# Fifteen rows of the first tile's expert sum scaled and added by GpSimd between its gathers, where VectorE added eleven

## What is computed

```python
def peer(h, w_query, sub_keys, expert_u, expert_v):
    ...
        idx = jnp.take_along_axis(cand_i, best_pos, axis=-1)
        gate = jax.nn.softmax(best_s, axis=-1)
        u = expert_u[idx]
        act = jax.nn.gelu(jnp.einsum('thkd,td->thk', u, x_blk), approximate=False)
        vsel = expert_v[idx]
        return jnp.einsum('thk,thkd->td', (gate * act).astype(vsel.dtype), vsel)
    ...
h = h + mix
h = h + peer(rmsnorm(h, norm_ffn[i]), ...)
```

## Time and profile before

| | us |
|---|---|
| median of 3 executions | 1581.6 |
| lowest, highest | 1579.9, 1583.37 |
| the profiled execution, its own time | 1584.37 |
| its span, first to last instruction | 1582.4 |

### The profile page before, as it was taken

The page is one execution under the profiler, slowest core; times in us unless marked ns, Lnnn a source line. Parts: engine busy times, 40 slices in busy tenths (PEclk is TensorE's granted clock), DMA queues, the critical chain, the costliest instruction groups (busy, mean ns, idle before and its releaser), DMA issues.

```text
span 1582.4 us, 14473 instructions
## 1 busy us (share of the span) xinstructions
PE 1348.0 (85%) x4096; PEld 666.3 (42%) x4096; DVE 973.4 (62%) x2432; ACT 537.7 (34%) x1639; POOL 564.0 (36%) x532
## 2 busy tenths in 40 slices
PE   7999899889775997889998699788899887777776
PEld 5555465445332443333565244333365432332222
DVE  3327498988774444763477755574557788554544
ACT  2324232323233223562323323564322323332322
POOL 1001355464342332434443233344333343343330
PEclk9999999999998999989999899999999999899999
DMA  9317999999999999999999999999999999999995
GB/s 382 142 53 292 371 405 421 421 421 421 421 421 422 420 421 421 419 404 409 421 421 421 420 421 422 421 407 386 423 421 420 422 420 422 422 421 422 421 421 218
DMA packets 85230, 620.39 MB, mean 392 GB/s; under 512 B 10368, under 2 KB 10368, under 8 KB 11424
## 3 DMA queue, kind: packets, MB, share of 16 engines
q0 software_dynamic: 74768, 551.65, 84.3%
q1 hardware_dynamic: 9792, 67.51, 10.4%
q10 hardware_dynamic: 592, 0.31, 0.1%
HBM read 618.38 MB, written 1.05 MB: 391 GB/s over the span
## 4 chain that ended last, share of the span: by engine, by line
PE 41%; DMA 39%; DVE 9%; ACT 7%; issue 3%; SPq 0%; POOL 0%; ACTq 0%; DVEq 0%; POOLq 0%
DMA arena<-in_peer_uv_dram,hnT 28%; PE banks L544 25%; DMA raw<-in_peer_uv_dram,hnT 6%; PE banks L571 5%; PE banks L424 5%; DMA work<-in_peer_uv_dram,hnT 3%; DVE arena L1430 3%; PE banks L692 2%; DMA rt<-in_diff_lambda_k_dram 2%; ACT g_e L934 2%; ACT hnT L923 1%; PE banks L516 1%; DMA spare<-in_peer_uv_dram,hnT 1%; DVE raw L1430 1%; ACT hnT L918 1%
## 5 line engine op out<-in xcount | busy, mean ns | idle before, releaser
L544 PE MATMUL banks<-arena,g_e 128*128 128x512 f32 x1184 | 576.6, 621 | 129.2 <-ACT g_e L934 127.7
L350 POOL DMA_INDIRECT arena<-in_peer_uv_dram,hnT x299 | 321.2, 1074 | 510.4 <-PE banks L544 498.5
L544 PEld LDWEIGHTS banks<-arena,g_e 128*128 128x128 f32 x1184 | 218.2, 196 | 404.6 <-issue 216.9
L1430 DVE CUSTOM_DVE_ANT_0 arena<-arena,hrows 128x1024 f32<-128x1024 f32 x209 | 254.1, 1223 | 154.5 <-DMA arena<-in_peer_uv_dram,hnT 148.3
L918 ACT ACTIVATE hnT<-hnT 128x2 f32<-128x2 f32 (+2 forms) x241 | 48.9, 203 | 698.6 <-DVE hnT L1430 698.4
L544 PE MATMUL banks<-raw,g_e 128*128 128x512 f32 x424 | 207.1, 620 | 40.2 <-ACT g_e L934 36.3
L350 POOL DMA_INDIRECT raw<-in_peer_uv_dram,hnT x106 | 116.5, 1099 | 180.5 <-PE banks L544 178.4
L934 ACT ACTIVATE g_e<-ident,hnT 128x128 f32<-128x128 f32 x501 | 172.8, 393 | 1.9 <-ACT hnT L923 0.6
L1430 DVE CUSTOM_DVE_ANT_0 arena<-arena,banks 128x1024 f32<-128x1024 f32 x90 | 109.6, 1220 | 85.4 <-DMA arena<-in_peer_uv_dram,hnT 85.3
L544 PEld LDWEIGHTS banks<-raw,g_e 128*128 128x128 f32 x424 | 78.0, 196 | 132.5 <-issue 78.0
L1430 DVE CUSTOM_DVE_ANT_0 raw<-raw,hrows 128x1024 f32<-128x1024 f32 x80 | 97.5, 1223 | 56.7 <-DMA raw<-in_peer_uv_dram,hnT 56.6
(11 more groups left out here) (244 smaller groups left out, 1302.7 us busy)
## 6 DMA issues: line engine op xcount, KB each, us to landing
arena<-in_diff_in_dram SPq DMA_DIRECT2D x24, 1024.0 KB, 9.9
arena<-in_peer_query_dram SPq DMA_DIRECT2D x16, 1024.0 KB, 12.1
arena<-in_gla_in_dram POOLq DMA_DIRECT2D x5, 2048.0 KB, 20.6
arena<-in_peer_query_dram SPq DMA_DIRECT2D x4, 2048.0 KB, 10.5
arena<-in_diff_out_dram SPq DMA_DIRECT2D x8, 1024.0 KB, 10.1
arena<-in_peer_uv_dram,hnT POOLq DMA_INDIRECT x299
work<-in_gla_out_dram POOLq DMA_DIRECT2D x2, 2048.0 KB, 40.2
arena<-in_gla_in_dram SPq DMA_DIRECT2D x2, 1024.0 KB, 12.3
```

Of the source, the lines that this page charges most:

```text
L350: pool.indirect_dma_start(pair(n), None, table, bass.IndirectOffsetOnAxis(ap=places[:, o:o + 1].bitcast(u32), axis=0)).then_inc(S(f"pair_l ...
L544: last = nc.tensor.matmul(bank(2 * (tile % NT) + half), diags[:, slot * P:(slot + 1) * P], v_row(n)[:, half * 512:(half + 1) * 512], start ...
L1430: V.tensor_tensor_reduce(out=u_row(n), in0=u_row(n), in1=normed, scale=1.0, scalar=0.0, op0=ALU.mult, op1=ALU.add, accum_out=dots[:, o:o + ...
```

## The change

`ADDED` becomes fifteen rows, 3, 11, 19, ... 115. VectorE's `added` goes. GpSimd instead multiplies the `v` half in place with the weights and adds it onto `h[:, 0, :]`, right behind gather n+8 (behind gather 9 for row 3); the next gather is the one that writes into that row's buffer.

```diff
-ADDED = [n for n in range(16, 80, 6)]
+ADDED = [n for n in range(3, SLOTS - 8) if n % 8 == 3]
+ADD_BEHIND = {n + (6 if n < 8 else 8): n for n in ADDED}
...
                     ).then_inc(S(f"pair_loaded_{HOME[n]}"), 16)
+                late = ADD_BEHIND.get(n)
+                if late is not None:
+                    if added_to(late) > 1:
+                        pool.wait_ge(S("v_added"), added_to(late) - 1)
+                    pool.wait_ge(S("weighted"), late + 1)
+                    wait_landed(pool, late)
+                    pool.tensor_scalar(v_row(late), v_row(late), weights[:, late:late + 1], None, ALU.mult
+                                       ).then_inc(S("v_scaled"), 1)
+                    pool.wait_ge(S("v_scaled"), added_to(late))
+                    pool.tensor_tensor(h[:, 0, :], h[:, 0, :], v_row(late), ALU.add).then_inc(S("v_added"), 1)
...
-            def added(n):
...
-                    for n in ADDED:
-                        if SUM_T[n] == ticks:
-                            added(n)
```

More of the change, by code:

```diff
@@ L1432, in dot @@
                                        ).then_inc(S("u_dotted"), 1)
-            def added(n):
-                if added_to(n) > 1:
-                    dve.wait_ge(S("v_added"), added_to(n) - 1)
-                dve.wait_ge(S("weighted"), n + 1)
-                o = n % PICKS
-                V.scalar_tensor_tensor(out=h[:, 0, :], in0=v_row(n), scalar=weights[:, o:o + 1], in1=h[:, 0, :],
-                                       op0=ALU.mult, op1=ALU.add).then_inc(S("v_added"), 1)
             ticks = settled = 0
```

## The result

The changed kernel takes 1591.0 us (median of 6 runs, 1587.8 to 1592.65), the kernel before beside it 1582.6 us (6 runs, 1579.9 to 1583.4). The ratio is 1.0049 with an interval of 1.0038 to 1.0060: **slower by 8.4 us**. The forecast was 1584.9 us and the range ended at 1590.0, so it came out on the slower side, as the forecast had it, and two and a half times as far (8.4 us where the forecast added 3.3). The profiled execution took 1592.65 us with a span of 1590.7 us; before it was 1584.37 us with 1582.4 us.

The account below looks back on a forecast made before the run. The prediction took the DMA stream at 421 GB/s as the bound: 1581.6 us plus 3.3 at gather 20, with VectorE's lost additions and the other fourteen pairs at nothing, gave 1584.9 us; range 1581.2 to 1590.0.

Parts of the forecast that it names:

- the first term: At gather 20, row 11's scale and add (4.2 us alone) would widen the DMA hole by 3.3 us, ends 0.3 to 6.9.
- the prediction's hold-up: GpSimd's scale, add and next gather wait for VectorE's dots: 1.0 us on average, at best 0, at worst 3.3.
- the cover of 1.2 us: Transfers still queued ahead of gather 20 would hide 1.2 us of its 4.5 us delay.
- the second term: Row 3's pair delays gather 10 by about 4 us, covered by 12.4 us of transfer in gathers 5 to 9.
- if gathers 17 to 19 moved: Sign in the profile after that would show the prediction wrong: these gathers starting at other times than before.
- the third term: Later pairs cost nothing: cover is 4.5 us at gather 35 and 8.4 at gather 99, and GpSimd catches up between pairs.
- the 3.3: Lateness in us of the DMA stream after gather 20's hole, counted as extra cover for later pairs.
- Rival 2: VectorE becomes the first tile's bound, as GpSimd's reads hold up its dots: 1589 to 1591 us, chance 0.14.
- Rival 1: The pair is short or meets no dot, 2.8 to 3.5 us: 1582 to 1583 us, the same; chance 0.19.
- Rival 3: TensorE's relief from rows 3 and 11 shows, each giving 1.8 us back: 1578 us, chance 0.07.

Follow-up runs that it names:

- e1: Kernel before with no row added by VectorE or GpSimd, all 128 rows summed by TensorE; 1581.4 us, ratio 1.0003.
- e3: Changed kernel with only the eleven pairs from row 35 on; 1581.9 us, ratio 1.0001 against the kernel before.
- e9: Changed kernel with row 11's pair alone, between gathers 19 and 20; 1584.4 us, ratio 1.0015 against the kernel before.
- e5: Changed kernel, but VectorE adds the fifteen rows and GpSimd writes zeros six times in each pair's place; 1591.9 us, ratio 1.0056 against the kernel before.
- e5b: Changed kernel, but VectorE adds the same fifteen rows and GpSimd only gathers, without zeros; 1583.2 us, ratio 1.0012 against the kernel before.
- e2: Changed kernel with row 3's pair alone, behind gather 9; 1585.5 us, ratio 1.0029 against the kernel before.
- e4: Changed kernel without row 3's pair, the other fourteen kept; 1592.4 us, ratio 1.0068 against the kernel before.
- e10: Changed kernel with row 27's pair alone, between gathers 35 and 36; 1582.8 us, ratio 1.0003 against the kernel before.
- e11: Changed kernel without row 27's pair, the other fourteen kept; 1587.0 us, ratio 1.0025 against the kernel before.
- e6: Changed kernel, but ScalarE scales the fifteen rows and GpSimd only adds them; 1587.8 us, ratio 1.0041 against the kernel before.

## Why the prediction was wrong in size

The forecast's sum was 3.3 us at gather 20 and nothing anywhere else; 8.4 us were measured, past the upper end of the range. One term of the sum was too small, and two terms put at nothing were not nothing.

**Right: what bounds the kernel, and what the change takes away.** The DMA stream decides. e1 bears out that the eleven additions of VectorE are worth nothing, as the prediction had read from 418 and 421 GB/s. e3 shows that the late pairs are covered, as read from the landing times. The largest hole is at gather 20, as forecast, and e9 makes it alone; but it is not the only one.

**Wrong, the first term: the size of a pair.** The prediction bounded the scale by a memset and an affine select of 128 numbers at 0.8 to 1.5 us for 1024, and took 1.3. It measured 2.86, outside both ends. The error was the assumption that an operation with one operand costs about what those two did for each number: a memset of 1024 did take 0.955 us in e5 (inside the bounds), but the scale takes 2.79 ns per number, and the add, with two operands, less than that (2.35 us; taken 2.4, bounds 1.5 to 2.9). The Trainium skill's figure for the add (GPSIMD Engine Reference, section 3.1; an estimate of 2.25 us by it) agrees. With 2.86 + 3.39 (the add waited about 1 us for dots, as the prediction's hold-up had it), gather 20 moved by 6.4 us from the pair and not by 4.5. With the cover of 1.2 us that is a hole of 5.2, where the term said 3.3; the window of 200 to 212 us lacks 6.0 us more than before. The upper end of this term, 6.9 us, did hold. The cover was itself misread, the other way: the prediction took 2.1 us from the end of an issue to its bytes in an empty queue, by the mean rate of two windows, where the DMA records show 0.7 for gather 20 behind the hole, and with the 2.8 us of gather 20 before that makes a cover of 2.1, not 1.2. And e9, with this hole alone, is slower by only 2.0 us (0.8 to 4.1 by its interval), so the size of the pair explains the hole but not by itself the 8.4.

**Wrong, the second term: "row 3's pair costs nothing".** The step counted the transfers that stood ahead of gather 10, and these did cover it. What it left out was TensorE. It said that row 3's removal saves nothing, since TensorE then idles anyway; it didn't ask what a longer idle time does. With the dot of row 5 ending later (held by the scale in the changed kernel), TensorE idled for 4.63 us, ran on at a lower granted clock (0.89 against 1.00 in 156 to 188 us), and the projection that releases gathers 12 and up came 3.0 us late. The held dot isn't needed for that: in e5 no dot was held, and yet TensorE idled for 3.61 us, came back at the lower clock, and gather 12 started at 176.51, where it started at 173.31 in e5b. e2 puts the price of the place at 3.5 us (1.9 to 7.4 by its interval), by its times alone; its trace doesn't show the loss, and e4 shows no gain without the pair. So that the place wasn't free is shown, and by what path it cost time stays open. The prediction had named the sign for this, "if gathers 17 to 19 moved", as what would make it wrong; they moved by 3.0.

**Wrong, the third term: the later pairs' cover was read in the kernel before.** Cover of 4.5 us at gather 35 plus "the 3.3" was taken for a stream that had been late once. Measured, gather 35's first bytes came 3.6 us behind its issue's end, where they came after 4.8 before and after 5.8 in e10, and the catching up was slower than reckoned: a pair and eight gathers were put at 15.2 of 19.9 us, and from row 27's scale at 243.51 to row 35's at 261.97 they took 18.5. e10 and e11 give the price: the pair of row 27 costs 0.3 us alone (no different from nothing) and about 4 us with the others in place.

**The rivals.** Rival 2 gave 1589 to 1591 and the time was 1591.0, yet its mechanism is not what happened. VectorE is busy for 73.74 of 80 us in 280 to 360 and doesn't overrun there, and e5, where no dot is held, is as slow. That its number fits is chance. Its premise, that GpSimd holds up VectorE's dots as these hold up GpSimd, is true: 21 of 114 dots between 140 and 460 us are over 1.35 us, together 23.9 us longer, where none of 120 was before. The Trainium skill states it so (SBUF — State Buffer, section "Who interferes with whom"), and these rows agree that the two engines hold each other up. They don't bear out that whoever comes first keeps the port to its end, as the prediction gave it: the dot that began at 162.23, 0.5 us ahead of the scale, still took 2.71 us, and in e6 a dot ran from 196.05 to 199.98 around an add of 196.54 to 198.89. (The profile's times of GpSimd's operations are rough, so this is a doubt and not a proof.) The effect is seen to cost time in one place, the end of the search in e4. Rival 1 (a short pair) fell with the first term. Rival 3 (TensorE's relief shows) didn't come either: it named row 3's sum as being on the path of the output projection, and in the changed kernel the projection came later, not earlier.

**What stays open.** Why the places don't add up: alone they cost 3.5 (row 3), 2.0 (row 11) and 0.3 (row 27) us, together 8.4, but without row 3's pair 10.4. e4's waits explain where its gain went, not why it takes longer than the changed kernel; by the intervals it may not (7.6 to 13.8 us against 6.0 to 9.5). Nor is it known why e2's executions are slower than e1's (3.5 against -0.6 us) when the two traces start their gathers alike. And when TensorE's clock falls after an idle time isn't settled: the last column has idle times of 3.61 us and more, all followed by the lower rate, and of 1.66 and less, none; between them 2.27, 2.98 and 3.14 were, 2.56 and 3.12 were not. So how much of row 3's price the lower clock carries can't be given; e1 had it too and lost no time.

## What to carry to other kernels

A queue that feeds the bound is no idle engine: before work is put on it, ask how many transfers stand ready at each place and how long each instruction holds the next issue, for in e5 holding the queue alone made the whole loss, and the eleven places with more cover cost nothing (e3). Read the cover at a later place after subtracting what the earlier places of the same change have used, since a pair that is free by itself (e10) cost about 4 us with the others in place (e11). Measure an operation at its own size before summing with it: 2.86 us stood where the bounds from 128 numbers ended at 1.5. Look for the relief where the queue waits: here four additions on VectorE at 171 to 183 us, where it had been busy for 7.8 of 12 us, gave 3.0 us, while fifteen on GpSimd took 8.4.

## What the runs showed of the hardware

- GpSimd scaled 128x1024 float32 by a number per partition in 2.86 us, longer than it took for the add of two such operands (2.35 us) and three times a memset of that size (0.955 us).
- GpSimd's scale and add hold not only VectorE's dots (1.22 us, up to 3.36 in the changed kernel, 4.09 in e6) but short operations too: 2.17 us in e4 for a TENSOR_SCALAR of 128x32, otherwise 0.18. A dot that began before GpSimd's operation was lengthened as well (2.71 us, begun 0.5 us ahead). Memsets, which read nothing, held no dot in e5, but a CAST took 0.97 us under one in place of 0.19.
- After a pause of TensorE of 3.6 to 4.6 us ahead of row 4's sum, its four matmuls of 128x512 took 3.78 us in place of 1.98, in all three runs that had such a pause there.
- From the end of a gather's issue to its first bytes passed 0.7 us when the queue was empty (gather 20 in the changed kernel, an estimate from the DMA records), and 4.8 us for gather 35 before, behind a full one.
